# Two attentions on one core: the reciprocals of the exponent sums move to the head of VectorE's step

## What is computed

```python
def causal_block_attention(q, k, v, scale):
    for i in range(S // Q_BLOCK):                     # 128 queries at a time
        s = jnp.einsum('bhqd,bhkd->bhqk', q_i, k[:, :, :end]) * scale
        p = jax.nn.softmax(jnp.where(mask, s, NEG_INF), axis=-1)
        outs.append(jnp.einsum('bhqk,bhkd->bhqd', p, v[:, :, :end]))
...
    p = jax.nn.softmax(s, axis=-1)                    # selected blocks, then the same for the window
    o = g[0] * o_cmp + g[1] * o_slc + g[2] * o_win
```

## Time and profile before

| | us |
|---|---|
| median of 3 executions | 2354.28 (2352.17 to 2355.89) |
| profiled execution, its own time | 2350.58 |
| span of the profiled execution | 2348.7 |
| granted TensorE clock, mean over the span | 0.957 of full |
| attention of layer 0 | about 327 to 479.5 |
| selected and window attention of layer 1 | about 1379 to 1780 |

### The profile page before, as it was taken

The page is one execution under the profiler, slowest core; times in us unless marked ns, Lnnn a source line. Parts: engine busy times, 40 slices in busy tenths (PEclk is TensorE's granted clock), DMA queues, the critical chain, the costliest instruction groups (busy, mean ns, idle before and its releaser), DMA issues. The chain is left out here.

```text
span 2348.7 us, 32886 instructions
## 1 busy us (share of the span) xinstructions
PE 2126.0 (91%) x12717; PEld 1469.9 (63%) x12717; DVE 957.4 (41%) x2310; ACT 722.5 (31%) x1803; POOL 472.9 (20%) x615
## 2 busy tenths in 40 slices
PE   6998859999899999969999769998999989999994
PEld 3444436655688888844655536666665568888883
DVE  3996865422512111113232666666661242111120
ACT  4014555511111111121121856666672111111110
POOL 0001003321112222100000444444441001222211
PEclk8999969999899999989999879999999998999997
DMA  5000011031779999945000100010002157999995
GB/s 207 0 0 0 1 63 37 19 110 64 310 265 360 366 364 369 341 128 148 1 0 1 75 1 10 19 47 10 10 10 84 63 209 266 362 371 368 364 349 130
DMA packets 85586, 346.72 MB, mean 148 GB/s; under 512 B 14272, under 2 KB 19415, under 8 KB 68470
## 3 DMA queue, kind: packets, MB, share of 16 engines
q1 hardware_dynamic: 66998, 277.47, 30.7%
q0 software_dynamic: 18432, 67.12, 11.1%
HBM read 288.29 MB, written 60.47 MB: 148 GB/s over the span
## 5 line engine op out<-in xcount | busy, mean ns | idle before, releaser
L1570 PEld LDWEIGHTS experts_gu_ps<-experts_x_cols,moew_gate 128*128 128x128 f32 x2048 | 241.7, 194 | 34.3 <-issue 34.3
L1570 PE MATMUL experts_gu_ps<-experts_x_cols,moew_gate 128*128 128x128 f32 x2048 | 242.5, 277 | 4.6 <-DVE experts_x_cols L1607 4.6
L1570 PE MATMUL experts_gu_ps<-experts_x_cols,moew_up 128*128 128x128 f32 x2048 | 239.1, 275 | 0.0
L1570 PEld LDWEIGHTS experts_gu_ps<-experts_x_cols,moew_up 128*128 128x128 f32 x2048 | 233.8, 192 | 0.0
L1581 PE MATMUL experts_y_ps<-moew_down,experts_hid 128*128 128x512 f32 x512 | 230.5, 593 | 2.0 <-DVE trunk_x_rows L1663 2.0
L1108 POOL TENSOR_SCALAR nsaatt_probs<-nsaatt_probs,nsaatt_inv,trunk_gates_or_logits 128x384 f32<-128x384 f32 (+7 forms) x256 | 183.8, 732 | 211.6 <-DVE nsaatt_inv L1135 211.6
L1656 DVE TENSOR_TENSOR experts_sig<-experts_gu_ps,experts_sig 128x256 f32<-128x256 f32 x64 | 27.2, 425 | 439.9 <-ACT experts_sig L1619 439.9
L1079 ACT ACTIVATE nsaatt_probs<-nsaatt_probs,nsaatt_bias 128x384 f32<-128x384 f32 (+7 forms) x256 | 169.0, 667 | 10.1 <-DVE nsaatt_bias L1130 10.1
L1510 POOL DMA_INDIRECT x_kept<-trunk_x_rows,moe_index x64 | 101.4, 1585 | 308.9 <-DVE trunk_x_rows L1663 221.1
L1619 ACT ACTIVATE experts_sig<-experts_gu_ps 128x256 f32<-128x256 f32 x64 | 24.5, 383 | 416.3 <-PE experts_gu_ps L1570 416.3
L1581 PEld LDWEIGHTS experts_y_ps<-moew_down,experts_hid 128*128 128x128 f32 x512 | 92.5, 191 | 95.4 <-issue 95.4
(11 more groups left out here) (382 smaller groups left out, 3238.0 us busy)
## 6 DMA issues: line engine op xcount, KB each, us to landing
moew_gate<-in_moe_w_gate_dram SPq DMA_DIRECT2D x64, 1024.0 KB
moew_up<-in_moe_w_up_dram SPq DMA_DIRECT2D x64, 1024.0 KB
moew_down<-in_moe_w_down_dram SPq DMA_DIRECT2D x64, 1024.0 KB
trunk_x_rows<-in_x_dram SPq DMA_DIRECT2D x16, 512.0 KB, 4.8
x_kept<-trunk_x_rows SPq DMA_DIRECT2D x16, 512.0 KB, 2.6
h_rows<-out_h_rows SPq DMA_DIRECT2D x16, 512.0 KB, 2.6
trunk_x_rows<-x_kept SPq DMA_DIRECT2D x16, 512.0 KB, 7.2
l0b_w_in<-in_mix_w_in_dram SPq DMA_DIRECT2D x1, 5760.0 KB, 23.7
```

Source lines behind the costliest of these rows:

```text
L1570: last = pe.matmul(to, wm[:, c, half * P:(half + 1) * P], x_cols[:, s % 2, c, :], start=(c == 0), stop=(c == CHUNKS - 1))
```

## The change

In VectorE's loop the reciprocals of step s + AHEAD - 1 stand at the head of step s, ahead of the masks of step s + AHEAD. Before, they stood behind those masks and behind `add(s)`. Their number and their waits (the exponentials of the same step) stay as they are. Nothing else is edited, and the other engines' queues are the same.

```diff
                 for s in range(S):
                     ahead = s + AHEAD < S
+                    if s + AHEAD - 1 < S:
+                        for r in range(BR):
+                            inverse(s + AHEAD - 1, r)
                     if ahead:
                         mask(s + AHEAD, 0)
                         mask(s + AHEAD, 1)
...
                         mask(s + AHEAD, 2)
                         mask(s + AHEAD, 3)
-                    if s + AHEAD - 1 < S:
-                        for r in range(BR):
-                            inverse(s + AHEAD - 1, r)
                     if ahead:
                         biased(s + AHEAD, LAST)
                     if s + 1 < S:
                         copies(s + 1)
```

## The result

The changed kernel takes 2454.71 us (median, 2446.17 to 2458.73), the kernel before 2353.23 in the same comparison. The ratio is 1.042, with a 95% interval of 1.040 to 1.044: **slower by 101 us**. Forecast were 2430 and +76, with a range of 2396 to 2462. The profiled execution took 2458.73, the slowest of the four; its span is 2456.9.

A forecast was written before the change was run, and what follows sets the result against it. TensorE, busy 91% of the span and held up by VectorE's copies and masks, was the bound. Layer 1 +70, layer 0 +4, given back -2, clock +4: +76 us on 2350.58 is 2426.6, as median 2430, range 2396 to 2462.

The forecast's parts named there:

- An earlier reciprocal gives nobody anything: Layer 1: GpSimd scales a step 9 us before TensorE turns it, so earlier reciprocals gain nothing.
- Narrow steps: masks and add between the last exponential and the copy: Layer 1: masks and add now delay VectorE's copy, which TensorE's transposes await; 5.9 us in eight steps, 44 in all.
- Step 16: Layer 1, narrow: TensorE goes on at 1504.70 against 1502.91, +1.8 us, making its wait 1.64 + 1.8 = 3.4.
- Step 14: Layer 1, narrow: VectorE's copy is of the fourth group and nothing in the step waits for it; counted 0.
- Wide steps: 3.1 us in eight steps, 23 in all: Layer 1: the first mask waits for the exponentials, delaying TensorE by +0.1, +0.7, +1.0 and +1.3 us in four steps.
- These add up and do not overlap: Layer 1: narrow and wide losses sum to 9.0 us per eight steps, 67.5 over 7.5 periods, +70 with the chosen mask.
- first rival: Layer 1: narrow and wide losses overlap instead of adding, leaving 5 us a period, 2396 us in all; chance 0.13.
- Layer 0: +4: Layer 0's attention: next scores wait for late masks, +1.1 us in three pairs and perhaps 0.25 four times.
- Given back: -2: Wide steps: reciprocals no longer stand ahead of bias and copy, saving 0.15 us each where TensorE waits; -2 us.
- The clock: +4: Some new TensorE waits near 3.83 us lose the full clock; from nothing up to 40 us, taken as +4.
- second rival: TensorE's clock falls after most of the new waits: 2426 + 40, some 2470 us; chance 0.10.
- The Trainium skill's rule on gaps: TensorE: repeated gaps beyond a certain length cost the full clock again and again; median about 2466 us.

The follow-up runs named there:

- runs 5 and 6: Kernel before, with layer 1's reciprocals at the step's head but one step later: 2348.34 us; or last in the step, behind the copies: 2348.02 us.
- run 3: Kernel before with the change in layer 1 alone, only where VectorE's masks are of a narrow step (branch 0 up to 512 keys): 2427.38 us.
- Run 10: Changed kernel, but in layer 1 VectorE copies each step's last group of transposes instead of every fourth group: 2373.85 us.
- run 4: Kernel before with the change in layer 1 alone, only where VectorE's masks are of a wide step: 2385.83 us, ratio 1.0133.
- run 2: Kernel before with the reciprocals moved in layer 1's attention alone: 2440.87 us, ratio 1.0366.
- run 1: Kernel before with the reciprocals moved in layer 0's attention alone: 2360.23 us, ratio 1.0021.
- Run 8: Changed kernel with two transpose buffers, plus 16 idle transposes before each layer 1 wide-step group that waits for VectorE's copy: 2489.27 us.
- run 7: Changed kernel with two PSUM buffers for the transposes instead of three: 2498.24 us.

## Why the prediction was right, and where its size was off

*An earlier reciprocal gives nobody anything.* Right: runs 5 and 6 make them later and are faster.

*Narrow steps: masks and add between the last exponential and the copy.* Right. Step 16 stands 3.59 us for a forecast of 3.4, step 18 in run 3 3.35 for 3.1, and over the whole of layer 1 run 3 has 46.3 us more idle time for a forecast of 44. Run 10 shows the cause: without a copy of VectorE in the way, 81 us go. Step 14 was counted at 0 and had 0.35 in run 3.

*Wide steps: 3.1 us in eight steps, 23 in all.* Right to 0.1 us in each of four steps (run 4). But this was read from one alignment of groups. The other costs 3.8 to 4.3, and the whole is 33 us.

*These add up and do not overlap.* Wrong in part. Narrow and wide together (run 2) give 18 us less than their parts (runs 3 and 4). The prediction's first rival named such an overlap, at twice the size.

*Layer 0: +4.* Measured +4.5 in the changed kernel's trace and +4.3 in run 1's, +6 for the whole kernel of run 1.

*Given back: -2.* Not seen by itself.

*The clock: +4.* This is the term that was mis-sized most. I took the new waits of 3.1 to 3.4 us as short enough for the most part. In the steps 16, 18 and their like they were 3.37 to 3.96 us. Of the sign that I had named as being wrong in the clock, 0.5 for many stretches inside the attention, the trace is full: in the 3 us behind each of the seven new waits of this length it is 0.50 to 0.63. So the second rival, that the clock falls after most of the new waits, came in its mechanism for the longest of them, at a price below its 40 us. TensorE's busy time in eight steps, forecast as before (43.22), is 50.91 in the row with 0.86. The clock is lost in pairs with shorter waits too, and is 0.89 over the whole of layer 1's attention against 0.98 before.

So the account of layer 1 is this. Forecast were 70 - 2 + 4 = +72. Run 3 has 28 us more busy time in place of 4, run 4 has 33 us in place of 23, and the overlap takes 18 back. That gives 72 + 24 + 10 - 18 = +88; run 2's trace has +89.5 (398.6 to 488.1). The changed kernel's trace has +96.7, at a clock of 0.89 where run 2 has 0.91, and layer 0's 4.5 make it 101. That the forecast came as near as it did is partly luck: the overlap that it left out takes back about half of what the clock and the wide steps have more.

What the lower clock is worth by itself can only be bounded, since slow work also fills time in which TensorE would have waited. Four pieces of the record give a price for each us at half speed. Run 8 has 9 us for 52, 0.17. The changed kernel's executions, 2458.73 us at 0.935 and 2446.17 at 0.946, have 12.6 us for 0.011 * 2 * 2457 = 54, 0.23. Those of run 2, 2450.01 at 0.939 and 2436.83 at 0.947, have 13.2 us for 0.008 * 2 * 2440 = 39, 0.34. And run 2's trace has the same eight steps, of the same alignment, at two clocks:

```profile
1495.81:1554.42 58.61, 46.63 (x424) 33.10 (x422) 30.19 (x114) 32.61 (x90) 22.64 (x33) 0.94 0.03 10
...
1733.90:1795.35 61.45, 50.40 (x424) 35.27 (x422) 30.39 (x114) 32.60 (x90) 22.63 (x33) 0.86 0.03 10
```

That is 2.84 us for 0.08 * 2 * 60 = 9.6, 0.30. Layer 1's attention spends 0.11 * 2 * 495 = 109 us at half speed in the changed kernel, and spent 0.02 * 2 * 399 = 16 before; the 93 us between them are worth 16 to 32 us (an estimate, at 0.17 to 0.34), where the forecast had 4. The exact share stays open.

The Trainium skill's rule on gaps ("TensorE: Matmul & The Clock Gate", "HAM oscillation — how this bites in real kernels") put the median at 2466, my reading of the rows at 2430; the result lies between them. In this trace the repeated loss of the clock is real, and its price, 16 to 32 us by the estimate above, is below the 40 that went with the rule, as work at the lower clock partly lies where TensorE would have waited.

## What to carry to other kernels

In a queue that is written by hand, ask of each instruction that waits for another engine what stands behind it and who waits for that; an operation whose result has a step or more of lead belongs behind everything that others wait for, not in front, however long its own reader is shown waiting. Where one engine's work falls between two others' in a ring of buffers, give it the element that nobody reads next: the last group and not the first. And where such waits grow on TensorE and come again and again, look at the granted clock behind them and count it too, some of which other waits cover. Before a sum from one stretch is multiplied over a loop, look whether the other stretches are aligned like it.

## What the runs showed of the hardware

Waits of 3.37 to 3.96 us of TensorE, again and again, were followed by the lower clock (ten transposes in 2.37 us instead of 1.28 behind a wait of 3.59). Not only those: in the changed kernel the eight steps from 1570.21 to 1630.88 have no wait over 2.10 us and still a clock of 0.89, with waits of 0.75 and 1.69 us close together. In run 4, with waits up to 1.54 us, the same steps kept 1.00. One wait of 3.05 us in run 3 had 1.00 behind it. The executions of the changed kernel and of run 2 spread over 13 us in four, where the kernel before has 7 to 11 us over 11 to 23; those of run 3, with such waits too, over 3 us. From pair to pair in one trace such steps are done at clocks of 0.97, 0.89 and 0.86.

From run 7 to run 8, 448 idle transposes in TensorE's waits for VectorE's copies raised the clock of layer 1's attention from 0.91 to 0.96.
